# A hybrid decoder block on one core: the final norm's weights travel as one row, and their old home takes expert weights

## The reference

```
x  = x + merged @ w_out
h  = rmsnorm(x, norm_ffn)
# 32 experts (1024 -> 256 -> 1024), two per token, inside one of four groups
for wg, wu, wd, c in experts:
    acc += ((silu(h @ wg) * (h @ wu)) @ wd) * c[..., None]
x  = x + acc
out = rmsnorm(x, norm_final)
```

## Time and profile before

| what | us |
|---|---|
| median of 3 runs | 499.3 (499.15 to 499.9) |
| the profiled execution, own time | 500.79 |
| its span, first to last instruction | 499.0 |
| TensorE busy in it | 464.9 (93%) |
| VectorE busy | 209.9 (42%) |
| ScalarE busy | 89.4 (18%) |
| mean granted clock of TensorE | 0.976 of full speed |

### The profile page before, as it was taken

The page is one execution under the profiler, slowest core; times in us unless marked ns, Lnnn a source line. Parts: engine busy times, 40 slices in busy tenths (PEclk is TensorE's granted clock), DMA queues, the critical chain, the costliest instruction groups (busy, mean ns, idle before and its releaser), DMA issues.

```text
span 499.0 us, 6262 instructions
## 1 busy us (share of the span) xinstructions
PE 464.9 (93%) x2450; PEld 253.5 (51%) x2450; DVE 209.9 (42%) x499; ACT 89.4 (18%) x243; POOL 34.2 (7%) x58
## 2 busy tenths in 40 slices
PE   6999999999999999999999899999999979699583
PEld 2499745564555545544446756456363626145130
DVE  1573019928766668779323442213131212112013
ACT  1000006214342110100011612111121201011012
POOL 0700050400000011000012100000000000000001
PEclk9999999999999999999999989999999999979988
DMA  8999679316026019789993689999999999999942
GB/s 263 416 372 226 200 281 376 130 44 295 0 66 273 0 42 420 297 328 408 365 412 134 261 342 429 412 430 427 407 431 414 424 428 407 433 410 429 418 191 87
DMA packets 20860, 151.32 MB, mean 303 GB/s; under 512 B 2948, under 2 KB 3397, under 8 KB 14173
## 3 DMA queue, kind: packets, MB, share of 16 engines
q1 hardware_dynamic: 19296, 147.88, 73.2%
q0 software_dynamic: 1296, 2.92, 2.8%
q10 hardware_dynamic: 236, 0.08, 0.1%
HBM read 148.25 MB, written 2.62 MB: 302 GB/s over the span
## 4 chain that ended last, share of the span: by engine, by line
PE 75%; DMA 12%; SPq 5%; DVE 4%; issue 2%; ACT 1%; POOLq 0%; POOL 0%; DVEq 0%; ACTq 0%
PE bank L672 35%; PE bank L697 30%; DMA ring<-in_moe_gate_up 12%; SPq L459 4%; PE bank L1121 4%; PE bank L1094 4%; PE bank L703 2%; SPq L456 1%; DMA ring<-in_dense 1%; DVE ring L1608 0%; DVE nsa L1520 0%; DVE nsa L1995 0%; PE bank L1131 0%; DVE rt L1520 0%; POOLq L148 0%
## 5 line engine op out<-in xcount | busy, mean ns | idle before, releaser
L1995 DVE COPY nsa<-bank 128x512 f32<-128x512 f32 x32 | 22.1, 691 | 99.9 <-PE bank L672 77.6
L697 PE MATMUL bank<-ring,x 128*128 128x512 f32 x128 | 57.3, 594 | 0.0
L672 PE MATMUL bank<-ring,nsa 128*32 128x512 f32 x336 | 44.0, 648 | 9.0 <-DMA ring<-in_moe_gate_up 8.9
L697 PE MATMUL bank<-ring,hT_and_y 128*128 128x512 f32 x96 | 43.4, 597 | 0.0
L672 PEld LDWEIGHTS bank<-cst,nsa 128*128 128x128 f32 x256 | 31.2, 195 | 23.9 <-issue 18.8
L1454 ACT ACTIVATE nsa<-bank 128x512 f32<-128x512 f32 x32 | 19.1, 597 | 126.7 <-PE bank L672 107.9
L697 PEld LDWEIGHTS bank<-ring,x 128*128 128x128 f32 x128 | 23.8, 190 | 27.6 <-issue 27.5
L672 PE MATMUL bank<-cst,nsa 128*128 128x32 f32 x256 | 33.9, 282 | 0.8 <-DVE nsa L1995 0.8
L1121 PE MATMUL bank<-selection,Tb 128*128 128x128 f32 x256 | 31.5, 283 | 0.3 <-DVE selection L1924 0.3
L2005 DVE SCALAR_TENSOR_TENSOR cst<-cst,bank 128x64 f32<-128x64 f32 x32 | 7.1, 221 | 56.2 <-ACT cst L1462 56.2
L1121 PEld LDWEIGHTS bank<-selection,Tb 128*128 128x128 f32 x256 | 30.5, 198 | 0.4 <-issue 0.4
(11 more groups left out here) (256 smaller groups left out, 660.1 us busy)
## 6 DMA issues: line engine op xcount, KB each, us to landing
ring<-in_moe_gate_up SPq DMA_DIRECT2D x21, 2048.0 KB, 19.4
ring<-in_dense SPq DMA_DIRECT2D x17, 2048.0 KB, 11.8
hT_and_y<-in_moe_gate_up SPq DMA_DIRECT2D x6, 2048.0 KB, 20.8
vr_and_gr<-in_moe_gate_up SPq DMA_DIRECT2D x5, 2048.0 KB, 22.7
nsa<-in_moe_down SPq DMA_DIRECT2D x10, 512.0 KB, 20.5
windows<-in_moe_down SPq DMA_DIRECT2D x8, 512.0 KB, 20.1
qkT<-in_moe_down SPq DMA_DIRECT2D x8, 512.0 KB, 20.0
keys<-in_moe_down SPq DMA_DIRECT2D x7, 512.0 KB, 14.8
```

The costliest lines, as they stand in the source:

```text
L672: return nc.tensor.matmul(o, l, r, start=s, stop=e)
L697: ins = nc.tensor.matmul(o, l[:, k, :], r[:, k, :], start=first and k == 0, stop=last and k == n - 1, skip_group_check=True)
L1995: V.tensor_copy(dst, bank[k][:, src]).then_inc(emptied[k], 1)
```

## The change

Three edits belong together.

- The second halves get a tenth home, the `cst` columns that `nffn` used. The second half of expert 9 is loaded there early, where the load of the norm's weights stood, and from then on each second half is loaded one place earlier in the stream.
- `norm_final` is no longer spread by a DMA. One row of 4 KB is loaded into row 0 of a first-half home that no later expert needs (`DW[0][3]`, named keys in the profile).
- At the head of the last batch TensorE waits for this row and multiplies a row of ones by each half of it, jobs NF0 and NF1 in two banks. ScalarE copies both to `nf`, and VectorE's wait for the load becomes a wait for those copies.

The later rounds use homes 4 to 7 instead of 0 to 3, so that `nf` is left alone.

```
-SEG = dict(first=GATHER_N, body=BATCH_C + GATHER_N + DOWN_C, last=BATCH_C + DOWN_C)
+SEG = dict(first=GATHER_N, body=BATCH_C + GATHER_N + DOWN_C, last=FINAL_C + BATCH_C + DOWN_C)
...
-        DW = [[b[:, 0:D] for b in down_homes] + [nsa[:, 3072:4096]], [b[:, D:2 * D] for b in down_homes]]
+        DW = [[b[:, 0:D] for b in down_homes] + [nsa[:, 3072:4096]], [b[:, D:2 * D] for b in down_homes] + [cst[:, C_ROT:C_ROT + D]]]
+        nf = DW[0][3]
...
             first_dw(9, (0,))
+            sp.wait_ge(s_xr, len(PIECES))
+            first_dw(9, (1,))
             sp.wait_ge(s_seed, 4)
             first_dw(5)
-            sp.wait_ge(s_xr, len(PIECES))
-            vec(nf, a["norm_final"], s_nf)
...
                 for h in range(2):
                     sp.wait_ge(*step_full("body", f"O{h}.c", 0, b - 2))
                     last = (b - 2) * BE + NDW[h]
+                    if last + BE > NE and h == 0:
+                        sp.dma_start(nf[0:1, :], a["norm_final"].rearrange("(a n) -> a n", a=1)).then_inc(s_nf, 16)
                     for e in range(last, min(last + BE, NE)):
                         first_dw(e, (h,))
...
+                if seg == "last":
+                    pe.wait_ge(s_nf, 16)
+                    for h in range(2):
+                        o = start(f"NF{h}.c")
+                        end(f"NF{h}.c", mm(o[:, :], ones[0:1, :], nf[0:1, h * 512:(h + 1) * 512], True, True))
                 gate_up(0)
                 gate_up(1)
                 turn(0)
...
+                if seg == "last":
+                    for h in range(2):
+                        out_of(f"NF{h}.c", nf[:, h * 512:(h + 1) * 512])
                 out_of("GU1.c", gu_sb[:, 1, :])
...
+                else:
+                    for h in range(2):
+                        dve.wait_ge(*step_out(seg, f"NF{h}.c", r, 0))
                 out_of("O1.c", o_sb[:, 1, :])
...
-            dve.wait_ge(s_nf, 16)
             weighted(0)
```

More of the change, by code:

```diff
@@ L122 @@
 BATCH_C = ["GU0.c", "GU1.c", "T0.c", "GU2.c", "T1.c", "GU3.c", "T2.c", "T3.c", "WT.c"]
-GATHER_N, DOWN_C = ["G0.n", "G1.n"], ["O0.c", "O1.c"]
+GATHER_N, DOWN_C, FINAL_C = ["G0.n", "G1.n"], ["O0.c", "O1.c"], ["NF0.c", "NF1.c"]
 SUMMED = ((0, 0), (1, 0), (0, 1), (1, 1))
-SEG = dict(first=GATHER_N, body=BATCH_C + GATHER_N + DOWN_C, last=BATCH_C + DOWN_C)
+SEG = dict(first=GATHER_N, body=BATCH_C + GATHER_N + DOWN_C, last=FINAL_C + BATCH_C + DOWN_C)
 SEG_BANK0 = dict(first=len(BATCH_C) % 4, body=0, last=0)
@@ L248, in build @@
         nffn = cst[:, C_ROT:C_ROT + D]
-        nf = cst[:, C_ROT:C_ROT + D]
         rtmp = yaT[:, 0:2, :].rearrange("p a t -> p (a t)")
@@ L315, in build @@
         s_gu = [sem(f"gate_up_loaded{i}") for i in range(6)]
-        s_dw = [[sem(f"down_half{h}_loaded{i}") for i in range(n)] for h, n in enumerate((10, 9))]
+        s_dw = [[sem(f"down_half{h}_loaded{i}") for i in range(n)] for h, n in enumerate((10, 10))]
         s_out1 = sem("out1_loaded")
@@ L544, in one_round @@
                     for h in range(2):
-                        load_dw(h, j, j, 0)
+                        load_dw(h, j + BE, j, 0)
                 with sp.Fori(0, NB - 1) as b:
@@ L552, in one_round @@
                         for h in range(2):
-                            load_dw(h, j, j, b * BE + BE)
+                            load_dw(h, j + BE, j, b * BE + BE)
             rounds(sp, one_round)
@@ L1218, in weights @@
                         else:
-                            i, ks = j, (j, j)
-                            gu, dw = loads_before(NGU, j, r) + b + 1, [loads_before(n, j, r) + b + 1 for n in NDW]
+                            i, ks = j, (j + BE, j + BE)
+                            gu, dw = loads_before(NGU, j, r) + b + 1, [loads_before(n, j + BE, r) + b + 1 for n in NDW]
                         ws.append((GU[i], [DW[h][ks[h]].rearrange("p (k n) -> p k n", k=2) for h in range(2)],
```

## The result

| | before | changed |
|---|---|---|
| median, us | 499.6 (499.15 to 502.23, 4 runs) | 511.37 (510.68 to 512.74, 4 runs) |
| ratio, 95% interval | | 1.0228 (1.0192 to 1.0264) |
| profiled execution, us | 500.79 | 510.68 |
| its span | 499.0 | 508.8 |
| mean granted clock | 0.976 | 0.962 |

The change makes the kernel slower by 11.8 us at the median. 508.0 was forecast, in a range up to 511.0. The median lies 0.4 us above that range, while the ratio, 1.0228, times the 499.3 us of the forecast gives 510.7. A second set on another chip gave 1.0179 (1.0111 to 1.0247). A ratio here is taken from the runs in the faster of the chip's two states and is not the quotient of the medians beside it, from which it differs by up to 0.3%; one run of ten in experiment 7, and one of the kernel before in experiment 12, fell in the slower state.

The account below looks back on a forecast made before the run. The weight stream was taken to set the last batches' pace. Later transposes +8.3 (row's wait, products, batch), clock +1.7 and down(0) -1.3 sum to +8.7 us, taking the median from 499.3 to 508.0 us; range 504.6 to 511.0.

Parts of the forecast that it names:

- The place and the cause: Head of the last batch: TensorE waits 15.4 us for the 4 KB row queued behind expert 31's block; the main effect.
- Where the row lands: End of SP's queue: row issued at about 447.2 us lands with the slowest DMA engine at 476.4 us, like expert 31's block.
- a sign against it: Last batch: the prediction is wrong if TensorE's idle time ends well before the block of expert 31 lands.
- early-engine rival: Wait at the last batch's head: row on an early DMA engine, wait ends at 472.5 to 475, 504.1 to 506.6; chance 0.18.
- Point 1, the two products: Head of the last batch: two products for the norm cost 0.9 us, bounds 0.4 and 1.8.
- Point 2, the batch at full pace: Last batch: 11.1 us from first gate and up to transposes, which start at 488.4 instead of 480.08, +8.3 us.
- Point 3, the clock: TensorE after its idle time: a 3.4 us spell at half speed costs +1.7 us, bounds 0 and 3.4.
- Point 4, what is given back in `down(0)`: Last batch: down(0) escapes its low clock spell, 1.99 us instead of 3.26, -1.3 us, bounds -1.3 and 0.
- Point 5, the bytes: Weight stream: the removed 512 KB are worth 0, bound -0.5 if the first refill finds the engines sooner.
- Point 6, the copies: Last batch: ScalarE's two 0.60 us copies fall into gate_up(0) and gate_up(1) and cost 0; 1.2 if gate_up already waited.
- The sum: Whole kernel: 8.3 + 1.7 - 1.3 = +8.7 us, span 507.7, median 508.0.
- Batches 0 to 6 were to be unchanged: Batches ahead of the last: a sign of the forecast, unchanged to within 0.5 us.

Follow-up runs that it names:

- experiment 7: Changed kernel with the row still late, its wait and the two products moved to just before gate_up(3) of the last batch: 502.31 us, 1.0012 times the kernel before.
- experiment 12: Kernel before plus tenth home and both down halves of experts 28 and 29 behind expert 31's block, norm spread by DMA last: 496.49 us, ratio 0.9952.
- experiment 2: Changed kernel with the row issued by SP ahead of the gate and up blocks of experts 28 to 31: 500.79 us, 1.0008 times the kernel before.
- experiment 3: Changed kernel with the row issued by ScalarE's queue after its copy of down(0) of batch 5, not by SP: 500.2 us, 1.0012 times the kernel before.
- experiment 6: Changed kernel with twelve useless products put in TensorE's queue ahead of the wait for the row: 507.08 us, 1.0113 times the kernel before.
- experiment 1: The changed kernel again without edit, on another chip: 509.96 us, 1.0179 times the kernel before.
- experiment 5: Changed kernel with each of the two products for the norm made twice: 512.44 us, 1.0212 times the kernel before.
- experiment 4: Changed kernel without row, products and copies, the norm's weights spread by a 512 KB DMA at the row's place: 499.86 us, 1.0004 times the kernel before.
- experiment 9: Changed kernel, row first, products behind gate_up(0), second down halves of experts 28 and 29 behind expert 31's block: 497.41 us, 0.9913 times the kernel before.
- experiment 10: Changed kernel, row first, products behind gate_up(0), both down halves of experts 28 and 29 behind expert 31's block: 496.07 us, 0.9896 times the kernel before.
- experiment 11: Kernel before, without the change, with both down halves of experts 28 and 29 behind expert 31's block: 498.01 us, 0.9925 times the kernel before.

## Why the prediction was right, point by point

- **The place and the cause.** Right. The wait for the row stands at the head of the last batch, with at least the 8 MB of the last four blocks ahead of it in SP's queue, and experiments 2, 3 and 7 each take it away in another manner (issue order, queue, place of the wait) and land at 1.0008, 1.0012 and 1.0012.
- **Where the row lands.** The forecast put it with the slowest engine, at the block of expert 31. This step failed in detail: in four traces TensorE's wait for it ended 2.1 to 3.5 us before that block landed, 25.4 us behind its issue in the changed kernel where 29 was expected. The prediction had named an idle time that ends well before the block as a sign against it. That is the early-engine rival, to which 0.18 was given. By the Trainium skill, DMA: Bandwidth & Descriptors, section "Why a DMA increments its semaphore by 16 and not by 1", a transfer on few engines does not wait for the others; the lead agrees with that, and the reading that the row would be cut for 16 engines is not borne out. No trace shows the engine.
- **Point 1, the two products.** Mis-sized. 0.9 us was taken for two, with 1.8 as the bound; they take 1.9 us from start to start in experiment 2, and 3.7 at the low clock in the changed kernel. The eight rows are four products of the program, each in two records, and the prediction read them as eight. The order of TensorE's instructions under "The change", said there to have four rows for these sums, could have told it.
- **Point 2, the batch at full pace.** 11.1 us. Right: experiment 6 gives 14.7 us, which is 1.9 + 11.1 + 1.7.
- **Point 3, the clock.** Mis-sized: 1.7 us, with 3.4 as the bound. The low level held for 9.3 us behind the wait, and half of that is 4.65 us. Four traces agree on this price within 0.3 us. From the start of the products to the transposes it is 13.0 us and half of the time at the low level: 17.5 us with 9.3 low in the changed kernel, 16.1 with about 6.4 in experiment 1, 14.7 with 3.4 in experiment 6, and 20.4 with about 11.4 in experiment 5, whose products take 1.9 us more. How long a spell lasts is not fixed, so a forecast can only give a range for it.
- **Point 4, what is given back in `down(0)`.** Failed. A low spell came again, 490.3 to 497.0 us, twice as long as the one before the change, and what follows the transposes took 1.7 us more instead of 1.3 less. In experiment 1, the same kernel, the clock was at its full level there (1.00 from 485 to 500 us), so this term is chance, and its bound of 0 was too narrow.
- **Point 5, the bytes.** Right: experiment 4 gives 1.0004, and experiment 2, in which the 512 KB are gone as in the change, 1.0008. A small misreading: the DMA share is nine tenths in every slice of the earlier trace rows from 299.4 us on, not from 290; the slice before reads 8.
- **Point 6, the copies.** Right. ScalarE's copies stand at 472.80 and 474.50 us, 0.60 us each, and TensorE waits for neither.
- **The sum.** Batches 0 to 6 were to be unchanged to within 0.5 us, and the end of batch 6 came 1.9 us early, with the first refill. The low clock from 287 to 290 us (0.54 before) was absent in the trace after (1.00). That is the clock and not the change, since kernels with the tenth home that have the spell have their first refill at 291.5 us or later too. With these 1.9 us put back, the transposes come 8.13 + 1.9 = 10.0 us later than before, just as the forecast has it (8.3 + 1.7). This is luck: an earlier end of the wait (-3.8) hid the price of the products (+1.0) and of the clock (+2.8). Behind the transposes point 4 is off by 3.0, so the spans, again with the 1.9 us, differ by 11.7 us in place of 8.7. The medians of this set differ by 11.8; on the other chip the ratio of 1.0179 makes it 9 us.

## What to carry to other kernels

A small transfer is as late as its place in a full queue, here 25 us for 4 KB; what counts is where it is issued and how much of an in-order engine's work stands behind the wait for it. Move either and the loss is gone. When a weight stream sets the pace, ask which load TensorE needs last and let everything that is needed later be issued behind it: that gave 0.5 to 1.0% in experiments 9 to 12. The extra home by itself gave nothing that shows (experiment 4).

## What the runs showed of the hardware

- After 11.56 us of idle time TensorE worked 9.3 us at half clock; in the other trace of the same kernel it was about 6.4 us after 11.27 us of idle time. Useless products during the wait left 3.4 us of it and made the kernel faster.
- Where the clock is low just ahead of the refills, the weight stream starts 1 to 3 us later. In the fourteen traces the first refill stands at 289.90 to 290.59 us where the granted clock was 1.00 from 287 to 290 us, and at 291.50 to 292.79 where it was 0.50 to 0.66. The landing of the block of expert 31 follows it, 183.7 to 184.5 us behind in the ten traces in which the same loads stand ahead of it.
- The kernel before varied from 497.19 to 502.92 us over 25 runs on one chip. That the place of the low spells makes up part of this is likely and not shown, as these runs have no traces.
- A 128x512 float32 product, and also one with a single input row, leaves two records and takes 0.9 to 1.0 us at the full clock.
